# Summing the attention weights of the second query half on VectorE, and reading the last bounds from two pairs of banks

## The reference

```
s = q . k / sqrt(64) + c_q - c_k              # c: running sum of log-forget values
s = where(key position <= query position, s, -inf)
out = softmax(s) @ v
```

## Time and profile before

| | us |
|---|---|
| median of 3 runs | 1430.33 |
| the profiled execution | 1428.8 |
| its span | 1427.1 |
| TensorE busy | 1369.3 (96%) |
| VectorE busy | 1003.8 (70%) |
| ScalarE busy | 522.7 (37%) |
| projection and attention of the four pairs, with the start | 0 to 414 |
| LRU and output product | 414 to 668 |
| MLP | 668 to 1427 |

### The profile page before, as it was taken

How to read it: one execution, slowest core, us unless ns; L and a number is a source line. 1 busy time by engine, 2 the same in 40 slices (tenths; PEclk the granted TensorE clock), 3 DMA queues, 4 the chain that set the end, 5 groups by cost and what they waited for, 6 DMA issues and landing times.

```text
span 1427.1 us, 21431 instructions
## 1 busy us (share of the span) xinstructions
PE 1369.3 (96%) x7479; PEld 1168.0 (82%) x7487; DVE 1003.8 (70%) x1523; ACT 522.7 (37%) x964; POOL 389.7 (27%) x396
## 2 busy tenths in 40 slices
PE   5989999999899999999999999999999999999998
PEld 4765847839658887788999999999999999999997
DVE  6763453543624566765888898888888898888885
ACT  5224242342335555332532343334433343334330
POOL 5310101101100002101532454345433553255320
PEclk9999999999999999999999999999999999999999
DMA  6042333424343032012201110111101110121004
GB/s 200 12 115 74 89 80 111 106 65 113 77 128 84 3 105 87 33 47 89 60 6 53 59 59 27 32 59 59 47 12 59 59 59 0 59 59 59 0 30 133
DMA packets 129544, 92.90 MB, mean 65 GB/s; under 512 B 14678, under 2 KB 119126, under 8 KB 129492
## 3 DMA queue, kind: packets, MB, share of 16 engines
q1 hardware_dynamic: 129492, 92.20, 22.6%
HBM read 78.28 MB, written 9.71 MB: 62 GB/s over the span
## 4 chain that ended last, share of the span: by engine, by line
PE 85%; DVE 5%; DMA 4%; ACT 3%; issue 1%; POOL 1%; SPq 1%; DVEq 0%; POOLq 0%
PE psum L2043 16%; PE psum L2045 15%; PE psum L2044 15%; PE psum L2523 8%; PE psum L2525 8%; PE psum L2524 8%; DMA k_c<-in_cache_k_dram 3%; PE psum L2305 2%; PE psum L2256 2%; PE psum L2287 1%; PE psum L2290 1%; PE psum L2315 1%; PE psum L2414 1%; PE psum L2126 1%; DVE tops L1611 1%
## 5 line engine op out<-in xcount | busy, mean ns | idle before, releaser
L1909 DVE TENSOR_TENSOR mix<-mix,psum 128x512 f32<-128x512 f32 x660 | 417.8, 681 | 92.0 <-PE psum L2525 87.6
L2043 PE MATMUL psum<-h_hi,wu_hi 128*128 128x384 f32 x768 | 259.4, 338 | 0.9 <-DVE wu_lo L1874 0.9
L2045 PE MATMUL psum<-h_hi,wu_lo 128*128 128x384 f32 x768 | 258.1, 336 | 0.0
L2044 PE MATMUL psum<-h_lo,wu_hi 128*128 128x384 f32 x768 | 258.1, 336 | 0.0
L2523 PE MATMUL psum<-wd_hi,u_hi 128*128 128x512 f32 x516 | 201.3, 390 | 0.2 <-DVE mix L1909 0.2
L2525 PE MATMUL psum<-wd_hi,u_lo 128*128 128x512 f32 x516 | 200.7, 389 | 0.0
L2524 PE MATMUL psum<-wd_lo,u_hi 128*128 128x512 f32 x516 | 200.7, 389 | 0.0
L2043 PEld LDWEIGHTS psum<-h_hi,wu_hi 128*128 128x128 f32 x768 | 144.3, 188 | 10.0 <-issue 1.3
L2044 PEld LDWEIGHTS psum<-h_lo,wu_hi 128*128 128x128 f32 x768 | 144.3, 188 | 8.7
L2045 PEld LDWEIGHTS psum<-h_hi,wu_lo 128*128 128x128 f32 x768 | 144.4, 188 | 0.0
L1265 ACT CAST wd_hi<-raw 128x512 fp32r<-128x512 f32 x109 | 67.1, 621 | 179.7 <-PE psum L2525 81.2
(11 more groups left out here) (321 smaller groups left out, 2460.8 us busy)
## 6 DMA issues: line engine op xcount, KB each, us to landing
raw<-in_w_up_dram SPq DMA_DIRECT2D x32, 512.0 KB, 5.9
raw<-in_w_down_dram SPq DMA_DIRECT2D x32, 512.0 KB, 4.4
k_c<-in_cache_k_dram SPq DMA_DIRECT2D x32, 256.0 KB, 2.9
raw<-in_w_in_dram SPq DMA_DIRECT2D x32, 192.0 KB, 4.0
out_dram<-mix SPq DMA_DIRECT2D x9, 512.0 KB
v_c<-in_cache_v_dram SPq DMA_DIRECT2D x16, 256.0 KB, 4.2
raw<-in_w_in_dram SPq DMA_DIRECT2D x8, 512.0 KB, 5.4
raw<-in_w_out_dram SPq DMA_DIRECT2D x8, 512.0 KB, 4.1
```

The lines of the kernel that those rows point to most:

```text
L1909: nc.vector.tensor_tensor(half_of(t, half), half_of(t, half), psum[:, product_bank(n), :].rearrange("p (k n) -> p k n", n=P), op).then_inc ...
L2043: nc.tensor.matmul(out, hi(k), r_hi(k), start=first and k == 0, stop=False)
L2044: nc.tensor.matmul(out, hi(k), r_lo(k), start=False, stop=False)
L2045: last = nc.tensor.matmul(out, lo(k), r_hi(k), start=False, stop=end and k == n - 1)
```

## The change

The sums of the first half stay as they are (den_done now counts 3 in a pair, not 6). For the second half:

- `weight_sums` at u = 5, 7, 9 and 11 goes. VectorE instead adds the weights of each head up over the key tiles, in `shares` (one half for each head): 14 additions in a pair, two for each u = 5 to 11; u = 5 adds the slots of key tiles 0 and 1.
- `second_sums` on TensorE, behind `turn_past(p, 3)`, waits for all 14 and multiplies the two sums with `ones_s`, 512 columns each, into bank 7.
- `exp(s)` for s >= 14 waits for the values and the addition that read its slot, where it waited for the sums.
- SP's past values wait for `second_sums`, through den_done.
- `share_out(p - 1)`, which reads `shares`, moves ahead, to VectorE's tile 4 of the projection, between `norm(4)` and the low parts of tiles 0 to 3.
- The bounds (0,7) and (1,7) go to banks 0 and 1, so the low parts of tiles 4 to 7, which read these banks, come before them: those of head 0 at tile 8, ahead of `mean(8)`, those of head 1 behind `norm(8)`. The order is (0,6), (0,7), (1,6), shift 0, (1,7), shift 1. The turned maxima go to banks 2 and 3, so `turn_tops(hp, 1)` also waits for `exp(6 + hp)`; it stands for head 0 before bound (1,7), for head 1 between `scores(8)` and `scores(9)`.
- GpSimd fills one more block of zeros (64x512 of `dens`) at the start.

```
@@ BOUND_ORDER / BOUND_AFTER
-                   ("b", 1, 4), ("b", 0, 5), ("b", 1, 5), ("b", 0, 6), ("b", 1, 6), ("b", 0, 7), ("b", 1, 7),
-                   ("s", 0, 1), ("s", 1, 1)]
+                   ("b", 1, 4), ("b", 0, 5), ("b", 1, 5), ("b", 0, 6), ("b", 0, 7), ("b", 1, 6), ("s", 0, 1),
+                   ("b", 1, 7), ("s", 1, 1)]
-                   (1, 6): ("b", 0, 6), (0, 7): ("b", 1, 6), (1, 7): ("b", 0, 7)}
+                   (1, 6): ("b", 0, 6), (1, 7): ("b", 0, 7)}
+    W_ADDS = 14
+    def added_with(s):
+        hp, _, kt = attention_step(s)
+        return 2 * max(kt - 1, 0) + hp + 1
@@ bound_bank, turned_tops_bank
+        if t == 7:
+            return 0
-        return 6 + hp
+        return (6, 2)[qc] + hp
@@ SP
-                sp.wait_ge(den_done, 6 * p + 6)
+                sp.wait_ge(den_done, 3 * p + 3)
@@ GpSimd
+            n.link(nc.gpsimd.memset(dens[DH:P, 1, :], 0.0))
@@ ScalarE, exp(s), s >= 6
+                        if s < 14:
+                            act.wait_ge(den_done, 3 * p + (s - 6) // 4 + 1)
+                        else:
+                            act.wait_ge(pv_done, 12 * p + (s - 6) // 2 + 1)
+                            act.wait_ge(w_added, W_ADDS * p + added_with(s - 6))
@@ VectorE
+                def add_weights(u):
+                    for hp in range(2):
+                        s = 2 * u + hp
+                        _, qc, kt = attention_step(s)
+                        a0, a1 = step_queries(s)
+                        acc = shares[:, hp * SPAN + a0 - SPAN:(hp + 1) * SPAN]
+                        dve.wait_ge(exp_done, STEPS * p + s + 1)
+                        if kt == 1:
+                            if p >= 1:
+                                dve.wait_ge(mix_shared, p)
+                            first = pt[:, (s - 2) % 6, :]
+                        else:
+                            dve.wait_ge(w_added, W_ADDS * p + added_with(s) - 2)
+                            first = acc
+                        nc.vector.tensor_tensor(acc, first, pt[:, s % 6, 0:a1 - a0], ALU.add).then_inc(w_added, 1)
@@ VectorE, tiles of the projection
                     bounds_ahead(t)
+                    if t == NT - 1:
+                        low_queries(4, 0)
+                        low_keys(4, 0)
                     mean(t)
...
+                    if p >= 1 and t == 4:
+                        share_out(p - 1)
+                low_queries(4, 1)
+                low_keys(4, 1)
                 bound(0, 6)
-                low_queries(4, 0)
+                bound(0, 7)
                 bound(1, 6)
-                bound(0, 7)
-                low_queries(4, 1)
+                shift(0, 1)
                 bound(1, 7)
-                shift(0, 1)
                 shift(1, 1)
-                low_keys(4, 0)
-                low_keys(4, 1)
                 denominators(0)
+                add_weights(5)
...
-                for i in range(2):
+                for u in range(6, 10):
                     if not last:
-                        pair_lo(p + 1, 2 * i)
-                        pair_lo(p + 1, 2 * i + 1)
-                    else:
-                        lru_lo(0, i)
-                    sample_past(p, 2 * i + 1)
-                    if i == 0 and p >= 1:
-                        share_out(p - 1)
+                        pair_lo(p + 1, u - 6)
+                    elif u in (6, 8):
+                        lru_lo(0, (u - 6) // 2)
+                    add_weights(u)
+                add_weights(10)
+                sample_past(p, 1)
+                add_weights(11)
+                sample_past(p, 3)
                 denominators(1)
@@ TensorE
+                def second_sums():
+                    pe.wait_ge(w_added, W_ADDS * (p + 1))
+                    for hp in range(2):
+                        last = nc.tensor.matmul(psum[32 * hp:32 * hp + 32, 7, :], ones_s[:], shares[:, hp * SPAN:(hp + 1) * SPAN],
+                                                start=True, stop=True)
                     last.then_inc(den_done, 1)
...
-                meanwhile = {0: (0, 6), 1: (1, 6), 2: (0, 7)}
+                meanwhile = {0: (0, 6), 1: (0, 7), 2: (1, 6)}
                 for u in range(STEPS // 2):
                     if u == 3:
+                        turn_tops(0, 1)
                         bound(1, 7)
...
-                    if u % 2 == 1:
+                    if u in (1, 3):
                         weight_sums(u - 1)
...
                     if u == 3:
-                        turn_tops(0, 1)
+                        scores(8)
                         turn_tops(1, 1)
-                        scores(8)
                         scores(9)
...
                 turn_past(p, 3)
+                second_sums()
```

More of the change, by code:

```diff
@@ L279, in streaming_step @@
     o_copied, den_copied = sem("o_copied"), sem("den_copied")
+    w_added = sem("w_added")
     den_saved, den_cols_in, shares_saved, shares_in = sem("den_saved"), sem("den_cols_in"), sem("shares_saved"), sem("shares_in")
@@ L1112, in exp @@
                     if s >= 6:
-                        act.wait_ge(den_done, 6 * p + (s - 6) // 4 + 1)
+                        if s < 14:
[3 more added lines that the diff above has]
+                            act.wait_ge(w_added, W_ADDS * p + added_with(s - 6))
                     a0, a1 = step_queries(s)
@@ L1623, in denominators @@
                         dve.wait_ge(den_saved, 16 * p)
-                    dve.wait_ge(den_done, 6 * p + (2 if qc == 0 else 6))
+                    dve.wait_ge(den_done, 3 * p + (2 if qc == 0 else 3))
                     if qc == 0:
@@ L1629, in denominators @@
                     else:
-                        nc.vector.tensor_copy(dens[:, 1, :], psum[:, 7, :]).then_inc(den_copied, 1)
+                        nc.vector.tensor_copy(dens[0:DH, 1, :], psum[0:DH, 7, :]).then_inc(den_copied, 1)
+                def add_weights(u):
[13 more added lines that the diff above has]
+                        nc.vector.tensor_tensor(acc, first, pt[:, s % 6, 0:a1 - a0], ALU.add).then_inc(w_added, 1)
                 def bounds_ahead(t):
@@ L2250, in bound @@
                         pe.wait_ge(lo_done, NT * p + 4)
+                    if (hp, t) == (0, 7):
+                        pe.wait_ge(lo_done, NT * p + 8)
+                        pe.wait_ge(hi_done, HI_PAIR * p + 12)
                     for part in range(t // 4 + 1):
@@ L2262, in turn_tops @@
                 def turn_tops(hp, qc):
-                    pe.wait_ge(bound_read, 20 * p + ((4, 9)[hp] if qc == 0 else 18))
+                    pe.wait_ge(bound_read, 20 * p + ((4, 9)[hp] if qc == 0 else BOUND_ORDER.index(("b", hp, 7)) + 1))
+                    if qc == 1:
+                        pe.wait_ge(exp_done, STEPS * p + 7 + hp)
                     nc.tensor.transpose(psum[0:4, turned_tops_bank(hp, qc), 0:P], tops[:, hp, 4 * qc:4 * qc + 4],
@@ L2277, in scores @@
                     if s == 8:
-                        pe.wait_ge(lo_done, NT * p + 6)
+                        pe.wait_ge(lo_done, NT * p + 8)
                         pe.wait_ge(dup_in[1], 64 * p + 64)
@@ L2281, in scores @@
                         pe.wait_ge(bound_read, 20 * p + BOUND_ORDER.index(("b", 0, 5)) + 1)
-                    if s == 16:
-                        pe.wait_ge(lo_done, NT * p + 8)
                     if qc == 1 and kt == 0:
@@ L2314, in weight_sums @@
                         a0, a1 = step_queries(s)
-                        last = nc.tensor.matmul(psum[32 * i:32 * i + 32, 5 if qc == 0 else 7, a0 - qc * SPAN:SPAN], ones_s[:],
-                                                pt[:, s % 6, 0:a1 - a0], start=kt < 2, stop=kt >= 4 * qc + 2)
+                        last = nc.tensor.matmul(psum[32 * i:32 * i + 32, 5, a0:SPAN], ones_s[:], pt[:, s % 6, 0:a1 - a0],
+                                                start=kt < 2, stop=kt >= 2)
+                    last.then_inc(den_done, 1)
+                def second_sums():
[3 more added lines that the diff above has]
+                                                start=True, stop=True)
                     last.then_inc(den_done, 1)
```

## The result

The changed kernel takes 1421.5 us (median of 4 runs, 1418.7 to 1424.0) where the kernel before takes 1429.1 in the same comparison: 7.6 us less, ratio 0.9942 (95% interval 0.9927 to 0.9956). Taken again as the measure for the experiments it stands at 1422.0 us against 1430.5, ratio 0.9945 (0.9927 to 0.9963). The forecast was 1422.6. That sum is right, but some of its terms are not, and they err in opposite directions, so the closeness is luck in part; the experiments take them apart.

The account below looks back on a forecast made before the run. TensorE was taken to bound the kernel (85% of the span). Four pairs at 2.85 us win 11.4, share_out loses 3.7: 7.7 off 1428.8 is 1421.1, plus 1.5 for the median, 1422.6 us; range 1417.5 to 1427.5.

Parts of the forecast that it names:

- Step 1: Low parts ahead of mean(8): norm(8) and values(0) come 0.5 us later, which costs TensorE 0.5 us.
- Step 2: Bounds' new order at the head of the second half: 0.4 us a pair, not the 2.1 of the two waits.
- Step 3: Three sums of about 1.00 us go before block 1's turn, values(5) 0.3 us earlier: turn moves from 219.17 to 215.9.
- Step 4: Block 3 of the past keys waits for a 3.57 us DMA round: TensorE waits 1.05 us, before 0.28.
- Step 5: second_sums behind block 3's turn takes 1.01 us, adds no wait; block 5 at 223.4 against 226.25, 2.85 us won a pair.
- Step 6: VectorE's additions before second_sums, 0.61 us for 512 columns, are hidden and cost nothing, with 1.5 us to spare.
- the four things named: What stands behind a late addition: the copy of block 1, second_sums, the stream scores and SP's four past values.
- Step 7: share_out in tile 4 delays bound (0,2) by its full 1.22 us in pairs 1, 2 and 3: 3.7 us lost.
- The clock, left at one fall of four: Granted clock falls to 0.50 in one of four pairs, costing some 1.5 us; as sparse a stretch remains, so unchanged.
- the gaps in tile 6 and before block 3: The change's two new TensorE gaps, 1.45 us in tile 6 and 1.05 before block 3, could each bring another fall.
- the sum of 7.7: Whole kernel: 11.4 us won over four pairs, 3.7 lost to share_out, 7.7 us in all.
- The second rival: More falls of the clock in the new gaps: three at 1.5 us, 1427 us; chance 0.15.

Follow-up runs that it names:

- the bounds alone: Kernel before with only the change's bounds order, banks, turn_tops, scores(8) and low parts; sums, additions and share_out as before: 1426.1 us, ratio 0.9977.
- the doubled additions: Changed kernel with each of VectorE's additions of weights done twice (the second a maximum or the same sum): 1443.8 us.
- the pair of kernels with a quiet clock: Changed kernel with past-key turns earlier, low parts behind norm(8) and five unread products; share_out behind norm(4) 1412.1 us, ahead of mean(4) 1407.3 us.
- share_out, turns or low parts moved alone: Changed kernel with share_out ahead of mean(4), 1421.5 us; or turns of past-key blocks 0 to 2 one step earlier, 1416.7; or head 0's low parts behind norm(8), 1420.0.
- all three moved: Changed kernel with share_out ahead of mean(4), past-key turns of blocks 0 to 2 one step earlier, and head 0's low parts behind norm(8): 1410.4 us, ratio 0.9872.
- The fill: Changed kernel plus five unread 128x512 products, two before turn_tops(1,1), three before scores(9): 1417.2 us, ratio 0.9916.

## Why the prediction was right, and where it was not

**Step 1** (low parts, 0.5 us late): right; values(0) is 0.42 us later behind the first turn of the tops, undoing it gave 2.0 us.

**Step 2** (bounds, 0.4 us a pair): mechanism right, too small. Two shifts in one took 1.40 us and scores(9) came 1.85 us behind the turns of the tops (199.98, 201.83); now one shift is left there and it's 1.13 (203.03 to 204.16). The turn itself is as early as before; the gain is 0.66. The forecast was right that the 2.1 us of waits are not the gain.

**Step 3** (three sums gone): right. From the second turn of the tops to block 0 it's 15.38 us with the bounds alone (pair 0, 107.03 to 122.41) and 13.40 in the changed kernel's third pair, both at full clock: 1.98 us for the two sums in between.

**Step 4** (block 3 bound by the DMA's round): right in kind, the first term that was off in size. The round took 3.21 to 3.50 us in pairs 1 to 3 for the 3.57 taken from the earlier trace rows, and the waits were 0.47 to 0.76, not 1.05. In pair 0 it took 4.47, because this keys' DMA landed 3.7 us after its issue and not 2.5 to 2.8; the five profiles with the late turns and single additions have 1.47 to 1.85 us of wait there, so it's systematic. What in pair 0 delays it stays open.

**Step 5** (second_sums 1.01 us, no wait added): right at full clock, 1.05 us, 0.98 to the next product. By steps 2 to 5 a pair wins 2.85 us. Measured on pairs without a fall, first turn of the tops to block 5's turn: 52.55 us before (173.70 to 226.25), 49.28 after (268.25 to 317.53, the second of two turns in a row, 0.43 behind 317.10): 3.3 us.

**Step 6** (additions hidden): right. 0.60 to 0.64 us each in a row for the 0.61 forecast; they cost nothing. The slack was 1.5 us by the forecast; in the trace the last addition ends 1.6 us ahead of `second_sums` (222.09, 223.69), and the doubled additions had 0.9 to spare. What gives way first is the copy of block 1, one of the four things named.

**Step 7** (share_out costs 3.7 us): right, the most certain step of all; 1.20 us in each of three pairs, 4.7 us by the pair of kernels with a quiet clock.

**The clock, left at one fall of four: wrong.** This is the step that failed. In the seven profiles with the new order and the late sums and without a fill, 19 of 28 heads fall: 15 of 20 in the changed kernel (twice) and with share_out, turns or low parts moved alone, 2 of 4 with all three moved, 2 of 4 with the doubled additions. The bounds alone have 3 in 4. For the kernel before there is one profile, with 1 in 4, but the mean clock of the unprofiled runs goes the same way: 0.9908 over six runs of the changed kernel, 0.9934 over eleven of the kernel before beside them, two stretches of half clock by 0.0012 each. It doesn't put them on the bounds' order, since with that alone the mean was 0.9935 against 0.9917; which part of the change brings them is open.

I had argued that the new stretch is as sparse as the old one, and by its sum it is: in the 4 us ahead of scores(9) TensorE is busy 2.26 us, where 290 to 294 us had 2.11. In the changed kernel it's 2.26 or 2.27 in all four pairs, and the third keeps the clock. The same share of busy time can thus keep the clock or lose it. The fill (no fall in 12 heads) shows that this stretch makes the falls; why one head falls and the next doesn't is open. What I cited from the Trainium skill, "TensorE: Matmul & The Clock Gate", HAM oscillation, I took to the gaps in tile 6 and before block 3 as places of new falls; in tile 6 there is none, before block 3 there's one, in pair 0, where the gap is 1.7 us. Its general sense, that gaps bring the half clock, the fill bears out.

So the sum of 7.7 was met by errors of opposite sign, which is luck: the pairs win 3.3 us and not 2.85, 1.8 more in all, and the half clock (two more falls at 0.9 to 1.35 us, and 1.6 us in pair 0) gives back some 4. With share_out these terms leave 4 x 3.3 - 3.7 - 4 - 1.2 (pair 0's DMA) = 4.3 us. They are read from the two first profiles, and these lie 4.9 us apart (1427.1 and 1422.2), not 7.6: the profiled execution of the changed kernel is the slowest of its four. Between the first turn of the tops and the last turn of the past keys the two are 5.95 us apart (338.96, 333.01), 1.6 more than the terms give, and these stay without a row; ahead of that the changed kernel lost 1.7 us (81.08, 82.75), 1.2 of them against its own second profile, and behind it won 0.6. There the code is the same, and the eleven profiles without doubled additions follow the clock: 1005.4 and 1005.9 us without half clock around 575 us, 1006.3 to 1007.3 with 3.4 us of it, 1007.4 with 6.8. The second rival (more falls, 1427) was right in its mechanism and wrong in its sum.

## What to carry to other kernels

An operation that moves out of idle time costs its duration at the new place if the engine runs there without a gap: find that in the timeline before moving it, since a few us to the left it may be free, as here. A wait for a DMA's round is shortened by moving the instruction that issues it, not the one that waits. Where the granted clock falls behind a stretch of short waits, a few useless products in these waits can be worth more than a tuned order.

## What the runs showed of the hardware that was not expected

The half clock came, in 19 of 28 heads, behind a stretch in which no single gap was over 0.9 us, at 2.26 us busy of 4 in the changed kernel, and five products of 128x512 in it kept the full clock in 12 of 12 heads (three kernels). Where TensorE stood 1.73 us for a DMA in pair 0, and up to 4.4 us for VectorE with doubled additions, the work behind it ran at half clock as well; behind the 1.85 us of the third pair in the kernel with share_out moved, and behind 1.57 us in pair 0 with the low parts moved, it did not. The DMAs of past keys that are issued one by one behind the turns (256 KB each) landed in 2.5 to 2.9 us mostly, but one in 3.5 to 3.9 at the same place of every profile with the late turns and single additions; those of blocks 6 and 7, issued two at a time, took 4.1 to 5.7 (changed kernel). One of these last made TensorE wait 1.85 us, in the kernel with share_out moved; the other waits for them were 0.15 to 1.3 us long.
